# One-hots for four tokens at a time, smaller coefficient chunks, and other due slots in a one-core decoder layer

## The reference, cut to what matters

```
h    = rmsnorm(x, g_norm1) * (1 + sc1) + sh1           # adaLN from c
q, k, v, u, g = split(h @ w_in)                        # 2048 -> 5 x 1024
att  = dilated attention over q, k, v (and over cache_k, cache_v for the samples)
mix  = concat(att, gelu(u) * spatial_mix(layernorm(gelu(g))))
x    = x + gt1 * (mix @ w_out)
h2   = rmsnorm(x, g_norm2) * (1 + sc2) + sh2
# PEER: 8 heads, each picks 16 of 128 x 128 = 16384 experts per token
top  = two top-16 lists of (h2 @ w_query) . sub_keys, then the top 16 of their 256 sums
gate = softmax(top sums)
act  = gelu(expert_u[idx] . h2)                        # 128 slots per token
ffn  = sum over slots of gate * act * expert_v[idx]
y    = rmsnorm(x + gt2 * ffn, g_final)
```

## Time and profile before

| what | before |
|---|---|
| median of 3 runs | 3847.0 us (3837.4 to 3849.1) |
| the profiled execution | 3847.0 us, span 3845.3 us |
| PE busy | 3097.3 us (81%), mean clock granted 0.893 |
| DVE busy | 2419.0 us (63%) |
| ACT busy | 474.8 us (12%) |
| DMA | 1332.2 MB, mean 346 GB/s |

### The profile page before, as it was taken

One profiled execution on the slowest core, in us unless ns is written; L12 is line 12 of the kernel. 1 busy time (PEld: TensorE's weight loads), 2 busy tenths in 40 slices (PEclk: granted clock), 3 DMA queues, 4 the chain that ended last, 5 costly groups with the idle time before them and its releaser, 6 DMA issues.

```text
span 3845.3 us, 28891 instructions
## 1 busy us (share of the span) xinstructions
PE 3097.3 (81%) x9975; PEld 1872.0 (49%) x9975; DVE 2419.0 (63%) x4252; ACT 474.8 (12%) x989; POOL 1049.2 (27%) x779
## 2 busy tenths in 40 slices
PE   4899997979993577686883481469999889999996
PEld 1333443833342333333662251347677557777774
DVE  3110215885886765657899778986577638656655
ACT  0000201121212244301112000110000000000000
POOL 3000001232223322232423424223233214322330
PEclk8999998979996688898995596679999999999998
DMA  9999556888896799988977999789999979999994
GB/s 314 398 357 368 213 186 249 338 324 339 327 340 264 301 420 419 419 315 328 348 274 250 354 417 360 273 319 418 419 418 418 417 270 418 417 418 418 418 409 188
DMA packets 291907, 1332.23 MB, mean 346 GB/s; under 512 B 26553, under 2 KB 51129, under 8 KB 179273
## 3 DMA queue, kind: packets, MB, share of 16 engines
q0 software_dynamic: 106912, 749.72, 49.1%
q1 hardware_dynamic: 156442, 537.25, 36.5%
q10 hardware_dynamic: 28408, 43.42, 3.1%
HBM read 1290.49 MB, written 38.96 MB: 346 GB/s over the span
## 4 chain that ended last, share of the span: by engine, by line
PE 62%; DMA 18%; DVE 14%; issue 3%; ACT 1%; POOL 0%; SPq 0%; ACTq 0%; DVEq 0%; POOLq 0%
PE ps L1024 30%; PE ps L827 9%; PE ps L618 7%; DMA arena<-in_expert_u_dram,arena 6%; DVE arena L2156 6%; PE ps L777 4%; DMA arena<-in_cache_k_dram 3%; DMA arena<-in_expert_v_dram 3%; PE ps L709 3%; DMA arena<-in_w_in_dram 2%; DMA arena<-in_w_ada_dram 2%; PE ps L606 2%; DVE arena L2052 2%; PE ps L576 1%; PE ps L820 1%
## 5 line engine op out<-in xcount | busy, mean ns | idle before, releaser
L1024 PE MATMUL ps<-arena 128*128 128x512 f32 x3072 | 1364.7, 606 | 99.6 <-DMA arena<-in_expert_v_dram 82.8
L2156 DVE CUSTOM_DVE_ANT_0 arena<-arena 128x2048 f32<-128x2048 f32 x544 | 1241.1, 2288 | 316.3 <-DMA arena<-in_expert_u_dram,arena 311.6
L2430 POOL DMA_INDIRECT arena<-in_expert_u_dram,arena x544 | 796.4, 1464 | 1784.9 <-DVE arena L2156 1533.8
L1024 PEld LDWEIGHTS ps<-arena 128*128 128x128 f32 x3072 | 961.8, 315 | 498.0 <-issue 163.9
L2082 DVE SCALAR_TENSOR_TENSOR arena<-arena 128x2048 f32<-128x2048 f32 x158 | 371.7, 2353 | 206.5 <-issue 165.8
L827 PE MATMUL ps<-arena 128*128 128x512 f32 x896 | 404.4, 605 | 0.0
L1016 PE MATMUL ps<-arena 128*128 128x128 f32 x768 | 166.6, 360 | 201.5 <-DVE arena L2054 200.8
L2430 POOL DMA_INDIRECT arena<-in_expert_v_dram,arena x160 | 210.2, 1314 | 402.3 <-DVE arena L2082 357.7
L618 PE MATMUL ps<-arena 128*128 128x512 f32 x640 | 289.7, 606 | 9.5 <-DMA arena<-in_w_in_dram 9.5
L576 PE MATMUL ps<-arena 128*128 128x128 f32 (+3 forms) x954 | 163.8, 324 | 151.4 <-DVE arena L1950 30.2
L827 PEld LDWEIGHTS ps<-arena 128*128 128x128 f32 x896 | 167.9, 193 | 240.0 <-issue 230.8
(11 more groups left out here) (246 smaller groups left out, 1820.0 us busy)
## 6 DMA issues: line engine op xcount, KB each, us to landing
arena<-in_expert_v_dram SPq DMA_DIRECT2D x296, 512.0 KB, 9.1
arena<-in_w_ada_dram SPq DMA_DIRECT2D x96, 1024.0 KB, 10.6
arena<-in_w_in_dram SPq DMA_DIRECT2D x80, 1024.0 KB, 8.8
arena<-dense_coefs SPq DMA_DIRECT2D x27, 1536.0 KB, 13.8
arena<-in_w_query_dram SPq DMA_DIRECT2D x36, 1024.0 KB, 10.4
arena<-in_w_out_dram SPq DMA_DIRECT2D x32, 1024.0 KB, 5.2
arena<-in_cache_k_dram SPq DMA_DIRECT2D x24, 1024.0 KB, 17.2
arena<-in_cache_v_dram SPq DMA_DIRECT2D x24, 1024.0 KB, 25.6
```

The lines of the kernel that those rows point to most:

```text
L1024: ins = MM(ps[:, BANK[half, b] + c, :], weights, dense_v[m % V_DENSE][:, c * NC:(c + 1) * NC], start=(m == FIRST_TILE[half, b]), stop=(m = ...
L2156: V.tensor_tensor_reduce(out=u_slot[s % RING], in0=u_slot[s % RING], in1=h2[b], scale=1.0, scalar=0.0, op0=ALU.mult, op1=ALU.add, accum_ou ...
L2430: nc.gpsimd.indirect_dma_start(out=slot, out_offset=None, in_=table, in_offset=bass.IndirectOffsetOnAxis(ap=idx, axis=0),).then_inc(loaded ...
```

## The change

Six things change together.
- **One-hots.** DVE makes both one-hots of four tokens in one comparison of 1024 elements a partition (one TENSOR_TENSOR, `is_equal`). The coefficient is no longer multiplied in there: ACT scales the first one-hot in place, by one ACTIVATE of 128x128 for each token, and PE waits for ACT (`hot_scaled`) instead of for DVE. Buffers are still two, now of a quad each, and lie at another address.
- **Due slots.** A quarter of the input projection is due every 2.4 slots instead of 1.8 (96 slots instead of 72), a sample every 3.6 instead of 6.6 (29 instead of 53). `T_OUT` moves from 203.4 to 202.8, so all behind it keeps its slots.
- **One-hots' steps.** Block 0 has the same slots (132 to 247). Block 1's end at 288 and not at 307. Block 2's end at 399 and not at 404. All 64 early tiles are due by slot 383, ahead of block 2's one-hots at 385.5.
- **Tiles.** `EARLY_TILES` goes from 40 to 64, so that 320 tiles are loaded, not 296 (12.6 MB more). `JS` goes from 8 to 4: chunks of half the size, three in a ring, and six buffers for values instead of four. SP's loads are sorted by a key.
- **The end.** `T_LOW` is 474, not 470. What DVE and ACT did for blocks 0 to 2 behind the slot loop is now a program in it (`end_high`), due at slots 534 to 540: at slot 534 DVE waits for the last tile.
- **Semaphores.** Six semaphores of the first stage become two.

The diff, cut:

```diff
-JS = 8
+JS = 4
-V_DENSE = 4
-EARLY_TILES = 40
-PAIRS = P // 2
+V_DENSE = 6
+C_RING = 3
+EARLY_TILES = 64
@@
-    return T_IN + 1.8 * (4 * i + q)
+    return T_IN + 2.4 * (4 * i + q)
@@
-    return T_S + 2.0 + 6.6 * (n // H) + (0.6 * h if h < 4 else 4.5 + 0.6 * (h - 4))
+    return T_S + 2.0 + 3.6 * (n // H) + (0.4 * h if h < 4 else 2.0 + 0.4 * (h - 4))
@@
 C_FROM = [131.0, 258.0, 385.5]
-C_STEP = [1.8, 0.75, 0.27]
+C_STEP = [3.6, 0.9, 0.4]
...
-T_LOW = 470
+T_LOW = 474
+T_HIGH = 534
@@ PE, build_dense
+                    for q in range(QUADS):
+                        yield t_quad(b, q) + 0.4 * C_STEP[b]
+                        n = QUADS * b + q
+                        pe.wait_ge(hot_scaled, 4 * (n + 1))
+                        if n >= 2:
+                            pe.wait_ge(quad_taken, n - 1)
+                        for i in range(4):
+                            ins = MM(ps[:, n % 2, i * P:(i + 1) * P], one_hot[n % 2][:, 1, i * P:(i + 1) * P],
+                                     one_hot[n % 2][:, 0, i * P:(i + 1) * P], start=True, stop=True, skip_group_check=True)
                         ins.then_inc(hot_used, 1)
@@ ACT, build_dense
+                    for q in range(QUADS + 1):
+                        if q < QUADS:
+                            yield t_quad(b, q) + 0.2 * C_STEP[b]
+                            n = QUADS * b + q
+                            act.wait_ge(hot_ready, n + 1)
+                            for i in range(4):
+                                hot = one_hot[n % 2][:, 0, i * P:(i + 1) * P]
+                                A.activation(hot, hot, ACT.Copy, scale=slot_t[:, 0, 4 * q + i:4 * q + i + 1]).then_inc(hot_scaled, 1)
+                        if q == 0:
+                            continue
+                        yield t_quad(b, q) + 0.3 * C_STEP[b]
+                        n = QUADS * b + q - 1
...
+                        act.wait_ge(hot_used, n + 1)
@@ DVE, build_dense
-                        for i in range(2):
-                            t = 2 * g + i
-                            V.tensor_scalar(one_hot[n % 2][:, i, 0, :], iota_key, slot_t[:, 1, t:t + 1], slot_t[:, 0, t:t + 1],
-                                            ALU.is_equal, ALU.mult)
-                            ins = V.tensor_scalar(one_hot[n % 2][:, i, 1, :], iota_key, slot_t[:, 2, t:t + 1], None, ALU.is_equal)
-                        ins.then_inc(hot_ready, 1)
+                        wide = [P, 2, 4, P]
+                        V.tensor_tensor(one_hot[n % 2].rearrange("p i (t n) -> p i t n", n=P),
+                                        iota_key.unsqueeze(1).unsqueeze(1).broadcast_to(wide),
+                                        slot_t[:, 1:3, 4 * q:4 * q + 4].unsqueeze(3).broadcast_to(wide), ALU.is_equal).then_inc(hot_ready, 1)
@@ DVE, in the slot loop (ACT's squares, roots and stores move likewise)
+            def end_high():
+                for b in range(DENSE):
+                    yield T_HIGH + b
+                    if b == 0:
+                        dv.wait_ge(tile_used, len(TILES))
+                    end_half(1, b)
+                yield T_HIGH + 3.5
+                for b in range(DENSE):
+                    mean(b)
+                yield T_HIGH + 5.0
+                for b in range(DENSE):
+                    scale_rows(b)
@@ SP
+            loads = [(CHUNK_AT[max(u - C_RING + 1, 0)] + V_DENSE - 1 if m < EARLY_TILES else
+                      max(CHUNK_AT[max(u - C_RING + 1, 0)], EARLY_TILES) + V_DENSE - 1, 0, u) for u, m in enumerate(CHUNK_AT)]
+            loads += [(m, 1, m) for m in range(len(TILES))]
```

More of the change, by code:

```diff
@@ L1501, in _ @@
                 side.upto(s)
-            for b in range(DENSE):
-                act.wait_ge(fin_x[0], 2 * (b + 1))
-                if b >= 2:
-                    act.wait_ge(fin_sq[0], b - 1)
-                square(b, 0, at(VD0 + D * (b % 2), D))
-            for b in range(DENSE):
-                root(b)
-            for b in range(DENSE):
-                store(b)
             act.wait_ge(y_stored, 16 * (BLOCKS + 1))
@@ L2041, in build_dense @@
                     V.tensor_copy(slot_keys, keys_int).then_inc(keys_split, 1)
-                    for g in range(PAIRS):
-                        yield t_pair(b, g)
-                        n = PAIRS * b + g
-                        if g == 0:
+                    for q in range(QUADS):
+                        yield t_quad(b, q)
+                        n = QUADS * b + q
+                        if q == 0:
                             dv.wait_ge(slot_t_done, b + 1)
@@ L2164, in _ @@
                 side.upto(s)
-            dv.wait_ge(tile_used, len(TILES))
-            for b in range(DENSE):
-                end_half(1, b)
-            for b in range(DENSE):
-                mean(b)
-            for b in range(DENSE):
-                scale_rows(b)
         @block.sync
@@ L2411, in _ @@
                     cols = slice(n * D + t * NC, n * D + (t + 1) * NC)
[L2412 to L2414 removed]
+                    pool.dma_start(mod_dram[:, cols], mod_row[n % 4][QUAD * t:QUAD * t + 1 + DECB, :]).then_inc(mod_stored, 16)
+            pool.wait_ge(mod_stored, 64 * 4)
             pool.dma_start(scale2_a, mod_dram[0, 4 * D:5 * D].partition_broadcast(P)).then_inc(mod2a_loaded, 16)
```

102 lines of the change are left out of this document (48 added, 54 removed).

## The result

| | before | after |
|---|---|---|
| median (lowest to highest), 4 runs each | 3848.1 us (3837.4 to 3854.0) | 3903.2 us (3893.5 to 3906.4) |
| ratio, 95% interval | | 1.0142 (1.0112 to 1.0172) |
| span of the profiled execution | 3845.3 us | 3904.5 us |
| PE's last dense tile done | 3809.9 | 3762.8 |
| from there to the end | 35.4 us | 141.7 us |

What follows compares the result with a forecast made beforehand. DMA (418 GB/s), PE or DVE bounds each stage. Steps give -35 us up to slot 385, then -31, +9, -8, +114: +49 on the 3845 us span, median 1.7 above, 3896 us; range 3835 to 3950.

Steps and rivals of the forecast that it cites:

- 1 input projection: Input projection: 24 more slots in the same work, three resources above 94% disturb each other, +15 us (0 to +40).
- 2 attention: Attention: six more quads lie in it, at most 1 us each, +5 us (0 to +15).
- 3 samples: Samples: 24 fewer gathers, 60 us of DMA, of which three quarters are gained, -45 us (-60 to -20).
- Step 4: Block 1's one-hots, where DVE is full: comparisons save 20 us, the chain through ACT gives some back, -14 us.
- Step 5: Early tiles: 24 more, 38 us of DMA, mostly finding room from 2140 to 2430, +4 us (-15 to +30).
- Step 6: Block 2's one-hots, 146 us before: 16 slots instead of 24 and cheaper comparisons, 115 us, so -31 us.
- Step 7: Low half: bytes and PE both end at about 570 us, DVE's 88.7 us wait gone, +9 us (-30 to +35).
- 8 high half: High half: 128 tiles at 5.17 us and a restart, 665 us where 673 were seen, -8 us.
- Step 9: The end: DVE waits some 220 us at slot 534, leaving 149 us behind the last tile, +114 us (+95 to +140).
- The one-hots on ACT: Rival in the one-hot stages: the chain through ACT is slower, 80 us over forecast at most, half gives 3936; chance 0.22.

Runs made afterwards that it cites:

- experiment 1: The kernel after with the end of blocks 0 to 2 put behind the slot loop again: 3798.4 us, ratio to before 0.9888.
- experiment 2: The kernel before with only the end of blocks 0 to 2 moved into the slot loop, due at slot 534: 3952.1 us, ratio 1.0283.
- experiment 3: The kernel after with the old due slots (1.8 slots a projection quarter, 6.6 a sample): 3931.2 us, ratio to before 1.0240.
- experiment 4: The kernel before with only the new due slots (2.4 slots a projection quarter, 3.6 a sample): 3820.7 us, ratio 0.9936.
- experiment 6: The kernel of experiment 1 with 40 early tiles instead of 64: 3787.9 us, ratio to before 0.9850.
- experiment 5: The kernel after with the old scalar comparisons on DVE and no scaling on ACT: 3918.0 us, ratio to before 1.0187.
- experiment 10: The kernel of experiment 1 with the reloads of x due at slot 412 instead of 402: 3801.1 us, ratio to before 0.9882.
- experiment 7: The kernel of experiment 1 with T_LOW at 468 instead of 474: 3771.8 us, ratio to before 0.9807.
- experiment 9: The kernel of experiment 1 with the old buffers (JS 8, V_DENSE 4, C_RING 2): 3813.3 us, ratio to before 0.9910.

## Why the prediction was right, and where it was off

The forecast of 3896 us (3835 to 3950) met 3903, and its main term was right in place, mechanism and size. That the total came within 8 us was in part luck: seven of the nine rows below are off by 8 to 18 us, in both directions. Each measured value is from one profiled execution on either side, so the rows up to slot 384 are good to some 10 us each. What the forecast was made of:

| step | predicted | measured | by |
|---|---|---|---|
| 1 input projection | +15 | +29 | PE's products of w_in end at 1182, not 1153 |
| 2 attention | +5 | -5 | 154 us for 159 |
| 3 samples | -45 | -47 | 263 us for 310 |
| output projection | none | -10 | 153 us for 164 |
| queries, 4, 5 to slot 384 | -10 | +8 | slot 384 at 2400.7, not 2424.7, sum -24 |
| 6 block 2's one-hots | -31 | -13 | first tile behind them at 2539.1, not 2576.2, sum -37 |
| 7 low half | +9 | -1 | 563 us for 565 |
| 8 high half | -8 | -9 | 660 us for 669 |
| 9 the end | +114 | +106 | 142 us behind the last tile for 35 |
| span | +49 | +59 | 3904.5 for 3845.3 |

- *Step 9* was the case. The wait at slot 534 was to be some 220 us and was 202, DMA 154 GB/s in it, and 149 us of work behind the tile were 142. That the adds would take 2.8 us each was a little high: the last 24 took 61 us (3825.4 to 3886.3), 2.54 each, 6 us less. Experiments 1 and 2 give its price on two kernels, 105 and 109 us by the medians; behind the last tile the traces have 106 and 112.
- *Steps 1 to 3.* The samples were right. The projection took twice the value taken, inside its bounds; no resource is full in it (PE 316, DVE 302 of 340 us, DMA 373 GB/s). That three shares of 0.9 in one stage disturb each other is the prediction's reason for it, and no run tests it. For steps 1 to 3, -25 was predicted and -22 measured in the sum; experiments 3 and 4 give 28 and 23 for the due slots as a whole.
- *Step 5* is mis-sized. The early tiles were put at +4, since 9.9 MB would find room and the start was sooner; experiment 6's lengths show 21 us, of the 38 that their bytes take at 418 GB/s.
- *Step 4* did not come as predicted. The comparison was to give 14 us in block 1. By experiment 5 it gives none there: from the end of the queries to slot 384 it takes 412 us with the old one-hots and 411 with the new, with DMA full in both (399 and 401 GB/s behind block 1's last one-hot). What gave back a part of step 5's 21 us, so that the row has +8, is not isolated.
- *Step 6* is mis-sized too, though right in its stage: the turns and products were 27 us shorter, but 16 of these were lost at once in the gap to the first tile, which the prediction had priced at nothing ("18 idle as before"). It had named the short runs and given them 5 us; the store took 13 more, and the load behind it 3 (experiment 10).
- *The one-hots on ACT* were not slower. ACT's four scalings take 1.28 us, 0.32 each (1.4 was taken), as the timeline of ACT in after shows for the last quad of block 2, and the comparison 1.22 us (1.20 was taken), as its line has it:

```profile
2499.58 1.27 ACT L1424 ACTIVATE arena<-arena 128x128 f32<-128x128 f32 x4
L2067 DVE TENSOR_TENSOR arena<-arena 128x1024 f32<-128x1024 f32 x96 | 116.3, 1220 | 34.5 <-PE ps L1015 30.0
```

  The Trainium skill (VectorE: DVE Perf Modes, "The perf-mode tier table") has a float32 operation on two tensors at single rate. The formula of the same page in the Trainium skill (VectorE: DVE Perf Modes, "The TRN2 errata — SBUF-src ops pay a fixed extra latency per instruction") gives an estimate of 1.22 us for it. The trace agrees with both. PE's eight products took 2.07 us and not 0.9 (the granted clock was 0.59 in that stage); PE was busy 57 of 136 us there. Its wait for ACT, 115.9 us, is smaller than the 200.8 us for DVE that it replaced.
- *Step 7* was right in its sum and wrong in its parts. DVE's wait was to be under 20 us, and was 57. The sum took it that tiles and gathers would end together, but slot 474 was there at 3040 with 24 of the 64 late tiles still to come. Their price of 3.79 us was the one spacing of the earlier trace rows; from 2882 to 3040 they came 4.55 us apart in the mean. Experiment 7 shows what that wait is: behind it the tiles get the whole DMA. Of the 83 us of PE time that 24 more early tiles save, the prediction had most "eaten there by the pace"; experiment 6 shows that all but 8 were.

By the medians the change splits as follows: the end +105, due slots -28, one-hots -15, chunks and buffers -15, early tiles +10, which makes +57 where +55 were measured. By the ratios, which take out that the kernel before ran 5 us apart in two of the batches, the same parts are +98, -38, -17, -8 and +15, which makes +49 or so. Each part is uncertain by some 10 us. `T_LOW` from 470 to 474 was not run alone; by experiment 7 it should be a loss of some 18 us (27 for six slots). So the parts neither prove nor exclude that share, and how they act on each other stays open.

## What to carry to other kernels

In an engine's in-order stream, a piece put ahead of the stream's end takes everything behind it hostage to its own wait: ask not only what the piece costs (22 us of folds here), but when its releaser comes and which queues (here the gathers) stop with the engine. To price it, date both ends (the slot that it is due at, and the last tile), and lay what is queued behind it on top of the releaser.

Where two loaders share a full DMA, making one of them stand for a while can be a gain, and loading something twice to save another engine's time can be a loss (here 21 us paid, 8 given back): in the stretch where DMA is full, count bytes first.

A comparison that takes away 61 us of an engine's work gives back only what lies on the path, some 15 us here.

One profiled execution dates events only as well as the kernel repeats them: two traces that agree at one date (3091 us in experiment 6) can hide two differences that cancel. Compare the lengths between events, and against several traces whose code is the same.

## What the runs showed of the hardware

- A store of 2 MB in runs of 512 B landed 22.4 us after its issue beside full gathers (rows of 8 KB), in runs of 1 KB 15.6 us at the same place. The medians over all twelve stores lie closer, 13.6 and 13.1 us; first experiment 1's kernel (512 B), then experiment 9's (1 KB):

```profile
DMA to landing us min/median/max: 10.0/13.6/50.1
```

```profile
DMA to landing us min/median/max: 8.3/13.1/47.6
```

- Beside gathers of 8 KB rows a full DMA was shared about two to one. By the DMA records of the traces, in experiment 9's kernel, with four buffers and loads in rows of 4 KB, the gathers moved 277 GB/s and the loads 139 (2895 to 3030); in after, with six buffers and coefficients in rows of 2 KB, 286 and 129 (2900 to 3030). Inside a chunk the tiles came 3.79 us apart with four buffers and with six, two tiles of after:

```profile
2963.11 2.08 PE L1023 MATMUL ps<-arena 128*128 128x512 f32 x4 [1.70 <-DMA arena<-in_expert_v_dram]
2966.90 2.08 PE L1023 MATMUL ps<-arena 128*128 128x512 f32 x4 [1.71 <-DMA arena<-in_expert_v_dram]
```

  With the chunk loads between them the mean was 4.55 us a tile in after (2882 to 3040) and 4.18 in experiment 9's kernel (2878 to 3042).

- An ACTIVATE of 128x128 in SBUF with a scale operand takes 0.32 us in a row of four, against 0.36 from PSUM.
